# Chunk waits moved to the unit that reads the chunk, and the first weight group asked for on ACT's own DMA queue

## The reference, cut to what matters

```python
proj = rms_norm(x) @ w_in                                 # split into latents, gates, q, k, v
o_mla = mla(...) * silu(gate_mla);  o_fox = fox(...) * silu(gate_fox)
o = concat([o_mla, o_fox]) @ w_out                        # 2048 x 2048
x = x + rms_norm(o, g_post)
x = x + 0.5 * (silu(n(x) @ w_gate) * (n(x) @ w_up)) @ w_down
# mixer: attention y_att and gated spatial branch y_sg, then
merged = sigmoid(g_att) * (o_att @ w_att_out) + sigmoid(g_sg) * ((u * spatial) @ w_sg_out)
x = x + merged @ w_out
x = x + 0.5 * (silu(n(x) @ w_gate) * (n(x) @ w_up)) @ w_down
return rmsnorm(x)
```

## Time and profile before

| | |
|---|---|
| time, median of 3 runs (lowest to highest) | 2650.59 us (2650.52 to 2651.16) |
| time of the profiled execution | 2646.32 us |
| its span | 2644.5 us |
| TensorE busy | 2611.7 us, 99% of the span |
| VectorE busy | 1494.1 us, 56% |
| ScalarE busy | 1186.9 us, 45% |
| GpSimd busy | 174.8 us, 7% |
| memory moved | 552.87 MB, mean 209 GB/s |

### The profile page before, as it was taken

The page is one execution under the profiler, slowest core; times in us unless marked ns, Lnnn a source line. Parts: engine busy times, 40 slices in busy tenths (PEclk is TensorE's granted clock), DMA queues, the critical chain, the costliest instruction groups (busy, mean ns, idle before and its releaser), DMA issues.

```text
span 2644.5 us, 32030 instructions
## 1 busy us (share of the span) xinstructions
PE 2611.7 (99%) x11785; PEld 2167.5 (82%) x11785; DVE 1494.1 (56%) x1700; ACT 1186.9 (45%) x1349; POOL 174.8 (7%) x292
## 2 busy tenths in 40 slices
PE   9999999999999999999999999999999999999998
PEld 8888778788888888888888888888788888888886
DVE  7755665755555555556655665555655555555554
ACT  5544553444444444444444554444444444444333
POOL 0110000000000000001100310000100000000000
PEclk9999999999999999999999999999999999999999
DMA  7876656577777776667876576665777777777554
GB/s 216 261 223 197 210 181 192 159 223 212 221 213 221 217 216 212 209 209 256 244 216 185 157 213 211 206 206 189 225 206 207 222 212 222 213 220 227 193 190 151
DMA packets 277138, 552.87 MB, mean 209 GB/s; under 512 B 21978, under 2 KB 24888, under 8 KB 276792
## 3 DMA queue, kind: packets, MB, share of 16 engines
q1 hardware_dynamic: 257520, 489.88, 60.7%
q0 software_dynamic: 19024, 61.54, 7.9%
q10 hardware_dynamic: 504, 0.26, 0.0%
HBM read 521.70 MB, written 29.89 MB: 209 GB/s over the span
## 4 chain that ended last, share of the span: by engine, by line
PE 98%; DVE 1%; issue 1%; ACT 0%; DMA 0%; SPq 0%; DVEq 0%; ACTq 0%
PE acc L547 95%; PE s_ps L675 1%; PE tr L587 1%; PE o_ps L698 1%; DMA raw<-in_w_in 0%; PE tr L903 0%; DVE act_lo L1380 0%; DVE merged_lo L1405 0%; DVE stats L1440 0%; DVE xres L1848 0%; ACT merged_hi L1019 0%; ACT whi L962 0%; DVE wlo L1348 0%; DVE xres L1838 0%; DVE xres L1567 0%
## 5 line engine op out<-in xcount | busy, mean ns | idle before, releaser
L1348 DVE TENSOR_TENSOR wlo<-raw,whi 128x1024 fp32r<-128x1024 f32 x929 | 1130.8, 1223 | 1003.8 <-ACT whi L962 1000.1
L962 ACT ACTIVATE whi<-raw 128x1024 fp32r<-128x1024 f32 x929 | 978.6, 1057 | 1174.2 <-PE acc L547 1158.4
L547 PE MATMUL acc<-whi,act_hi 128*128 128x512 f32 (+1 forms) x2560 | 692.7, 392 | 8.3 <-issue 7.0
L547 PE MATMUL acc<-whi,act_lo 128*128 128x512 f32 (+1 forms) x2560 | 682.9, 389 | 0.0
L547 PE MATMUL acc<-wlo,act_hi 128*128 128x512 f32 (+1 forms) x2560 | 682.7, 388 | 0.0
L547 PEld LDWEIGHTS acc<-whi,act_lo 128*128 128x128 f32 x2560 | 479.7, 188 | 100.1
L547 PEld LDWEIGHTS acc<-wlo,act_hi 128*128 128x128 f32 x2560 | 479.8, 188 | 99.6
L547 PEld LDWEIGHTS acc<-whi,act_hi 128*128 128x128 f32 x2560 | 473.3, 188 | 101.7 <-issue 9.3
L547 PE MATMUL acc<-wlo,h_hi 128*128 128x512 f32 x704 | 188.4, 389 | 0.0
L547 PE MATMUL acc<-whi,h_lo 128*128 128x512 f32 x704 | 188.4, 389 | 0.0
L547 PE MATMUL acc<-whi,h_hi 128*128 128x512 f32 x704 | 188.4, 389 | 0.0
(11 more groups left out here) (257 smaller groups left out, 1364.6 us busy)
## 6 DMA issues: line engine op xcount, KB each, us to landing
raw<-in_w_in SPq DMA_DIRECT2D x280, 512.0 KB, 4.4
raw<-in_ffn_w_gate SPq DMA_DIRECT2D x176, 512.0 KB, 4.4
raw<-in_ffn_w_up SPq DMA_DIRECT2D x176, 512.0 KB, 3.9
raw<-in_ffn_w_down SPq DMA_DIRECT2D x176, 512.0 KB, 4.6
raw<-in_w_out SPq DMA_DIRECT2D x64, 512.0 KB, 4.7
turn_dram<-h_turned POOLq DMA_DIRECT2D x25, 512.0 KB, 3.2
h_back<-turn_dram POOLq DMA_DIRECT2D x100, 128.0 KB, 5.6
raw<-in_w_sg_out SPq DMA_DIRECT2D x24, 512.0 KB, 3.8
```

What stands on the lines that cost most here:

```text
L547: return nc.tensor.matmul(pair[:, half, 0:width], left[:, k, half * P:(half + 1) * P], right[:, slot, t, 0:width], start=start, stop=stop, ...
L962: nc.scalar.activation(whi[:, slot, :, 0:width], raw[:, slot, :, 0:width], ACT.Copy).then_inc(hi_ready, 1)
L1348: nc.vector.tensor_tensor(wlo[:, slot, :, 0:width], raw[:, slot, :, 0:width], whi[:, slot, :, 0:width].bitcast(F32), ALU.subtract).then_in ...
```

## The change

In three places the count that makes the next unit wait is raised later, or at another place, and where the chunk isn't waited for by a unit's first matmul there is an explicit wait (`chunk_is_split`) ahead of the last chunk's transposes. In the opening SP no longer issues the first weight group; ACT does, behind the gains.

```diff
@@ SP, opening: in the loop over k, behind the loads of x
-                load(w_in, k, 0)
+                if k == 0:
+                    at.n["group"] += 1
+                else:
+                    load(w_in, k, 0)
@@ TensorE, gate units c = 0..3 and the first output-projection unit
-                    if c and j == 7:
-                        exchanged()
+                    if (c, j) == (3, 7):
+                        exchanged(CHUNKS - 2)
...
                     if c == 0 and j == 3:
+                        exchanged()
+                        chunk_is_split()
                         transpose_chunk(o_sb, 3 * W)
@@ TensorE, merge_chunk
                     if first_one:
                         if 1 <= j <= 6:
                             spatial(j - 1)
-                    if j == 6:
-                        exchanged()
+                        if j == 6:
+                            exchanged()
                 for j in groups(2, att_hi, att_lo):
                     pass
                 for j in groups(G_D, act_hi, act_lo):
-                    if first_one and j == 6:
-                        exchanged(SG_W // W)
+                    if j == 6:
+                        exchanged(SG_W // W if first_one else 1)
@@ TensorE, w_out_2 units
                     if j == 3:
                         if c == 0:
                             transpose_chunk(mixed)
-                        else:
-                            exchanged()
+                        elif c == CHUNKS - 1:
+                            exchanged(CHUNKS - 2)
@@ ACT, its first instructions
             act.dma_start(gain_rows[:], gains_by_row).then_inc(rows_in, 16)
+            act.dma_start(raw[:, 0], w_in[0:TILES * P, 0:W].rearrange("(t p) n -> p t n", p=P)).then_inc(raw_in[0], 16)
```

## The result

| | before | changed |
|---|---|---|
| time, median of 4 runs (lowest to highest) | 2650.88 us (2650.52 to 2651.42) | 2627.78 us (2627.73 to 2628.37) |
| profiled execution | 2646.32 us | 2627.8 us |
| its span | 2644.5 us | 2626.0 us |

The ratio of the timed runs is 0.9913 (95% interval 0.9896 to 0.993). That is 23.1 us less; 18.1 us were forecast, and the time lies 0.2 us under the range. The two profiled executions differ by 18.5 us.

The account below looks back on a forecast made before the run. TensorE's stream (99% busy) plus its holes was taken as the bound. 8.37 + 1.58 - 1.20 + 6.09 + 3.30 + 0 = 18.1 us, off 2650.6 us, gave 2632.5 us; range 2628 to 2639.

Parts of the forecast that it names:

- the last of the sum: Whole kernel: the timed median stays 4.3 us above the profiled time, so 2650.6 - 18.1 = 2632.5 us.
- the second rival: TensorE's clock: timed runs have two or three more falls behind the same waits, 3.2 to 4.7 us; about 2628; chance 0.10.
- The gate units: Ends of units c = 1, 2, 3: 8.37 us won without the chunk waits, 1.20 us lost waiting for the softmax twice.
- The 1.58 us for the clock: First group behind the third gate wait: without the idle stretch the clock stays up, 1.58 us won.
- The w_out_2 units and the merge loop: Three waits each: 2.03 us apiece in w_out_2, 6.09 us; 1.10 us apiece in the merge loop, 3.30 us.
- The explicit waits: Behind group 3 of the output projection and second feed-forward layer's first unit: cost nothing; 2.79 us if uncovered.
- The opening: First weight group issued by ACT: between 0.47 us won and 1.10 us lost, taken as 0.
- the first rival: Opening: input x comes late on shared transfer engines, up to 1.1 us lost, 2633.6 us; chance 0.12.
- The trace's sum as a whole: Profiled execution: all gains and losses together 18.1 us, from 2646.3 to 2628.2 us.
- The other rivals: Gate units give gains back, 2638.5 us, chance 0.13; units still wait, 2650, 0.03; weight stream late, 2660, 0.02.

Follow-up runs that it names:

- the earlier split: Kernel with the waits moved and the opening as before, with ACT and DVE splitting the gate units' exchanged chunk at j == 5 instead of j == 7: 2626.52 us.
- the control on one chip: Kernel with the waits moved, the gate units' chunk split at j == 5 and the opening as before, timed beside two kernels with other openings: 2626.75 us.
- The timed kernels with one edit each: Kernel before with only one place's waits moved: gate units 2639.48 us, w_out_2 units 2641.75 us, merge loop 2645.07 us, against 2649.68 us.

## Why the prediction was right about the change and wrong about the size

**What failed** is one step, the last of the sum: "The timed median is 4.3 us above the profiled time, which the trace does not explain; I take the same difference off it". The forecast so left 4.3 us standing above the profiled time of the changed kernel, and nothing stands there: 2627.8 us profiled and 2627.78 us timed. Most of the difference was no constant but falls of TensorE's clock behind the very waits that the change removes. They vary from execution to execution: one in the first profile, three in the second, 2.6 on average by the profiles and by the kernel that keeps TensorE at work. I had counted the one that the profile showed, 1.58 us, and named the rest as the second rival with a chance of 0.10.

The further 1.6 falls of an average execution are 2.5 us of the 4.6 by which the timed runs moved more. Another 1.2 us lie in the four executions that the result is compared with: their median is 2650.88 us, that of the 27 and of the 17 executions beside the later runs is 2649.7. The last 0.9 us stay open; waits such as the 1.17 us for the exchanged chunk are a candidate that the timed runs cannot show. So the rival had the mechanism, and that its time fits to the tenth is partly luck. Its own lower end, 2632.5 - 4.7 = 2627.8, is the measured time; the range was rounded to 2628, with no room below the rival that it ended on.

**The gate units**: 3 x 2.79 us less 2 x 0.60 us. The profile after shows the unit 2.78 us earlier behind its transposes and 0.54 us lost at the softmax. Right, and the earlier split shows the cause of the loss. The 1.58 us for the clock were right for the profiled execution.

**The w_out_2 units and the merge loop**: 6.09 and 3.30 us. The place and the cause are right, the starts in the profile after are one group apart, without a hole. The size was 0.9 us too small, 6.5 and 3.8 us: the forecast took 2.75 us for a group, a mean that holds the slower first group behind a wait, where a group without one takes 2.72, and it left out what that first group loses. The timed kernels with one edit each gave 7.9 and 4.6 us.

**The explicit waits** cost nothing, as said: the transposes at 384.04 follow the group before them with no wait.

**The opening** at 0 between 0.47 won and 1.10 lost: in profiles with the weights on ACT's queue the second group's matmuls start at 13.3 to 14.0, in those without at 12.7 to 13.7, with the moment at which the clock first rises mixed in. The direction is that of the first rival, x late. The page "DMA: Bandwidth & Descriptors" of the Trainium skill ("Queues, rings and completion order": the engines go round the queues) agrees with the rows: x's second half was taken up at 7.00 instead of 5.53, and at 7.39 where the control on one chip had both halves without a wait. The forecast set this against the section "Issuing engines are not separate DMA queues" of the same page; but that section of the Trainium skill, too, says that the transfers interleave on the same engines, so the two speak for the same side. In time it is too small to be measured here.

**The trace's sum as a whole**: 18.1 us forecast, 18.5 us between the two profiled executions. That it fits so well is in part luck: 0.9 us too little for w_out_2 and the merge loop stand against about 0.5 us that the profile after lost in the opening (9.62 against 9.07 at the first unit). The other rivals are out. The gate units did not give the time back, the accumulators held nobody, and of ACT's 1155.1 us of idle time ahead of the weight splits 1138.7 still end with TensorE.

## What to carry to other kernels

A semaphore that counts in order makes a reader wait for everything that was counted before; put the wait at the first instruction that reads the data, and ask at each unit's start what exactly it must have. When timed runs lie above the profiled execution, or spread in steps, profile it again and look for a state that one execution happens not to be in, before taking the difference for a constant: price each short stop of TensorE with its idle time and, on top, with the chance of a slow group behind it (here 9 in 15 for stops of 2.54 us, none in 15 for 0.97). Issuing a transfer on a second DMA queue did not bring it forward for free here: x, which shared the engines with it, came later, and it is worth asking which of the two is waited for.

## What the runs showed of the hardware

- TensorE's clock fell from its 2.4 GHz level to the 1.2 GHz level behind idle times as short as 2.54 us and 1.90 us, in some executions and not in others, at 1.5 to 1.6 us a fall. The same wait had one in one profile and none in the next (4.50 and 2.99 us for the same group at 323 us; 3.00 and 4.57 us at 380 us). In the profiles of the unfilled waits there were 9 falls in 15 idle times of 2.54 us, 4 in 15 of 1.90 us and none in 15 of 0.97 us.
- At the same clock the first group behind an idle time took 2.83 to 2.85 us instead of 2.72.
- With those waits gone the executions lay closer together: 5.4 us apart before (27 executions, 2646.6 to 2652.02), 0.6 us in the changed kernel (4 executions) and 0.5 to 1.4 us in the kernels built on it (5 each).
- TensorE waited 1.17 us for an exchanged chunk at 145 us in one profile, 0.41 us in another and not at all in both profiles of before.
- The moment at which the clock first rises varied as well: in two executions of the unchanged opening `keep_warm`'s 18 rows took 3.80 and 4.21 us.
